# Sums of squared keys and queries: one four-pass fp32 product replaced by two one-pass products of a high and a low part

## The chip, the cores and the metric

The kernel runs on one core of one Trainium2 chip. The metric is device time in microseconds (us) of one launch; lower is better. The engines are TensorE (PE: matrix products, with its weight loads listed as PEld), VectorE (DVE), ScalarE (ACT), GpSimd (POOL) and SyncE (SP, which issues most DMAs). Each has its own instruction queue that is worked in order, and they meet only at semaphores.

## The reference, cut to what matters

One encoder layer over 512 tokens (two groups of 256) with 1024 channels. The change sits in the first stage, which projects the normed input, convolves, applies SiLU, and L2-normalises keys and queries of the gated delta net, 8 heads of 128 channels each.

```python
n1 = rmsnorm(h, W['norm_mix'][i])
proj = n1 @ W['w_in'][i]
...
qkv = jax.nn.silu(centred_depthwise_conv(qkv, conv_w).astype(f32))
q, k, v = jnp.split(qkv, 3, axis=-1)
...
def l2norm(t):
    return t * lax.rsqrt(jnp.sum(t * t, axis=-1, keepdims=True) + EPS)
...
q, k, v = l2norm(heads(q)), l2norm(heads(k)), heads(v)
```

After it come a state-space mixer, the gated delta net, an expert feed-forward and an output gate, none of which the change touches.

## The kernel before, in words

The program is a row of stages (project, ssd, gdn, then the expert stages), each a block in which the five engines run side by side, with a barrier of all engines at its end. Only `project_stage` is changed.

In it the 5120 convolved channels are 40 tiles `t` of 128 channels, each `128 x 512` (channels on the partitions, tokens along the row). A pair of tiles shares one 128x2048 weight chunk. Exact fp32 products are avoided: every operand is split into a high part (`fp32r`, a rounded fp32 that TensorE takes in one pass) and a low part (the rest), and `products` adds high*high, low*high and high*low, 8 k-tiles times 3, so 24 matrix instructions for a tile (L180 to L182). The queues in one iteration `t` are written out by hand:

- **TensorE**: the 24 products of tile `t` into PSUM bank `t % 4`; then, for a key or query tile (head `k`, tiles 8 to 15 for `k` 0 to 7 and 24 to 31 for `k` 8 to 15), the sum of its squares, `LAG` = 2 tiles late (after product 10 for head 0, and so on): L517 multiplies the squares with a 0/1 column of `column_strip`, which adds the 128 channels of head `k` into row `k % 8` of PSUM bank 4. Then `spreads` (L492, the inverse norms sent back to all partitions) and the transposes of finished tiles (L536), where there are any.
- **ScalarE**: waits for product `t`, writes the centre tap of the convolution (L587); on odd `t` it then makes the high part of a coming weight chunk (L545, `split`); then SiLU of tile `t-1` (L557) and, for a head's tile, its squares (L563, into one of two slots of `squares_of`). So the head that follows a `split` is always an even `k`.
- **GpSimd**: makes the low part of each weight chunk as soon as its high part is there: L460, `w_low = w_slots - w_high`, one instruction of 128x2048, once in two tiles.
- **VectorE**: in iteration `t` copies a transposed tile (L649), scales a head by its inverse norm (L654), then waits for the centre tap and adds the three other taps (L683). Once for the keys and once for the queries it takes the reciprocal (L666) and makes the low part of the inverse norms (L669, a subtraction of two tiles in SBUF).

Of the kernel before, what the change touches and what calls it, by code (L numbers as in the profile page):

```python
# [7 lines left out]
ACT = mybir.ActivationFunctionType  # L8
AX = mybir.AxisListType
F32 = mybir.dt.float32  # L10
F32R = mybir.dt.float32r
U32 = mybir.dt.uint32

P = 128
SEQS = 2
L = 256
T = SEQS * L
# [99 lines left out]
def bits32(x):  # L117

    return x.bitcast(F32)
# [8 lines left out]
AT_XT, AT_OG, AT_CH, AT_WORK, AT_END = 57.25, 73.25, 89.25, 169.25, 222.5  # L128
# [199 lines left out]
def project_stage(nc, m):  # L328
# [10 lines left out]
    NH = GDN_H  # L339
    SQUARED = 2  # L340
    LAG = 2
# [4 lines left out]
    small_r, w_r, split_r = m.region(AT_XT, AT_OG), m.region(AT_OG, AT_CH), m.region(AT_WORK, AT_END - 4.25)  # L346
# [3 lines left out]
    wsh, wsl = small_r.take("w_small_high", [P, KT, 64], F32R), small_r.take("w_small_low", [P, KT, 64], F32R)  # L350
    tab = small_r.take("a_coefficients", [P, 48])
    small_t = small_r.take("small_t", [64, T])
    s2 = split_r.take("squares_of", [P, SQUARED, T])
    wh, wl = split_r.take("w_high", [P, 2, KT, CC], F32R), split_r.take("w_low", [P, 2, KT, CC], F32R)
    norms = split_r.take("norms_of", [P, T])
    norms_h, norms_l = (split_r.take(f"norms_{x}", [P, T], F32R) for x in ("high", "low"))
    strip = split_r.take("column_strip", [P, NH - 1 + P])
    rows = split_r.take("row_selectors", [P, NH, P], F32R)
    w_in = [m.sem(f"w_slot{j}_loaded") for j in range(2)]
    part_in = [m.sem(f"w_first{h}_loaded") for h in range(2)]  # L360
# [8 lines left out]
    squared, summed, rooted, inverted, spread, scaled = (  # L369
        m.sem(x) for x in ("qk_squared", "qk_summed", "qk_rooted", "qk_inverted", "qk_spread", "qk_scaled"))  # L370
    split_h, split_l = m.sem("norms_high_done"), m.sem("norms_low_done")
    made, zeroed = m.sem("selectors_made"), m.sem("strip_zeroed")
    turned, copied = m.sem("turned"), [m.sem(f"turned_copied_{x}") for x in ("act", "dve")]
    par = m.colp[:, COL_CONV:COL_MIX].rearrange("p (c k) -> p c k", k=5)
# [24 lines left out]
    def head_of(t):  # L399

        for n, c in enumerate(FIRST):
            if c <= t < c + NH:
                return n * NH + t - c
        return None
# [10 lines left out]
    with nc.Block() as block:  # L415
# [30 lines left out]
        @block.gpsimd  # L446
        def _(pool):
            pool.memset(m.eps[:, :], EPS)
            pool.memset(strip[:, :], 0.0).then_inc(zeroed, 1)
            pool.wait_ge(zeroed, 1)  # L450
            pool.memset(strip[:, NH - 1:NH], 1.0).then_inc(made, 1)
            for h in range(2):
                ks = slice(h * HALF, (h + 1) * HALF)
                pool.wait_ge(part_high, h + 1)
                pool.tensor_tensor(wl[:, 0, ks, :], w[:, 0, ks, :], bits32(wh[:, 0, ks, :]), ALU.subtract).then_inc(part_low, 1)
            pool.wait_ge(small_high, 1)
            pool.tensor_tensor(wsl[:, :, :], ws[:, :, :], bits32(wsh[:, :, :]), ALU.subtract).then_inc(small_low, 1)
            for c in range(1, CHUNKS):
                pool.wait_ge(high, c)
                pool.tensor_tensor(wl[:, c % 2, :, :], w[:, c % 2, :, :], bits32(wh[:, c % 2, :, :]), ALU.subtract).then_inc(low, 1)  # L460
                if c == 4:
                    pool.wait_ge(eye_in, 16)
                    pool.tensor_copy(rows[:, :, :], sq(m, "eye")[:, 0:NH].unsqueeze(2).broadcast_to([P, NH, P])).then_inc(made, 1)

        @block.tensor
        def _(pe):
            def tile_product(t, ready=lambda k: None):
                j = (t // 2) % 2
                f = slice((t % 2) * P, (t % 2 + 1) * P)
                if t >= 2 and t % 2 == 0:  # L470
                    pe.wait_ge(low, t // 2)
                if t >= BANKS:
                    pe.wait_ge(conv, t - BANKS + 1)
                products(pe, m.ps[:, t % BANKS, :], [(wh[:, j, k, f], wl[:, j, k, f]) for k in range(KT)],
                         [(m.nh[:, k, :], m.nl[:, k, :]) for k in range(KT)], ready).then_inc(prod, 1)

            def first(k):
                pe.wait_ge(norm.out_done, k + 1)
                if k % HALF == 0:
                    pe.wait_ge(part_low, k // HALF + 1)  # L480

            def spreads(t):
                for n in spreads_behind(t):
                    if n == 0:
                        pe.wait_ge(made, 2)
                        pe.wait_ge(act_small, 1)
                    if n % NH == 0:
                        pe.wait_ge(split_l, n // NH + 1)
                    if n >= 1:
                        pe.wait_ge(scaled, n if n <= NH else n - 1)  # L490
                    for last, part in enumerate((norms_h, norms_l)):
                        ins = pe.matmul(m.ps[:, spread_bank(n), :], rows[:, n % NH, :], part[:, :], start=last == 0, stop=last == 1)  # L492
                    ins.then_inc(spread, 1)

            pe.wait_ge(eye_in, 16)
            norm.pe(pe)
            for t in range(N_CONV):
                tile_product(t, first if t == 0 else lambda k: None)
                if t == 1:
                    pe.wait_ge(small_low, 1)  # L500
                    products(pe, m.ps[0:64, 6, :], [(wsh[:, k, :], wsl[:, k, :]) for k in range(KT)],
                             [(m.nh[:, k, :], m.nl[:, k, :]) for k in range(KT)]).then_inc(small_prod, 1)
                if t == 2:
                    pe.wait_ge(small_staged, 1)
                    for tt in range(TT):
                        last = pe.transpose(m.ps[:, 7, tt * 64:(tt + 1) * 64], small_t[:, tt * P:(tt + 1) * P], sq(m, "eye")[0:64, 0:64])
                    last.then_inc(small_turned, 1)
                k = head_of(t - LAG)
                if k is not None:

                    if k == 0:
                        pe.wait_ge(made, 1)
                    if k == NH:
                        pe.wait_ge(rooted, 1)
                    pe.wait_ge(squared, k + 1)
                    j = k % NH
                    pe.matmul(m.ps[:, 4, :], strip[:, NH - 1 - j:NH - 1 - j + P], s2[:, k % SQUARED, :], start=j == 0,  # L517
                              stop=j == NH - 1).then_inc(summed, 1)
                if t == DECAYS_AT:
                    pe.wait_ge(const_in, 32)  # L520
                    pe.wait_ge(dve_small, 1)
                    g = m.decay[:, :, 32:48]
                    for n, mask in enumerate(("le", "ge", "gt", "lt")):
                        last = pe.matmul(m.ps[:, 5, n * 64:(n + 1) * 64], sq(m, mask), g, start=True, stop=True)
                    last.then_inc(gate_out, 1)
                spreads(t)
                for g in turns_behind(t):
                    base, _, half, tt = turn(g)
                    if base == CH_K:
                        pe.wait_ge(scaled, 4 * half + 4)  # L530
                    else:
                        pe.wait_ge(active, base + 4 * half + 4)
                    if g >= 2:
                        pe.wait_ge(copied[g % 2], g // 2)
                    for a in range(4):
                        last = pe.transpose(m.ps[:, 6 + g % 2, a * P:(a + 1) * P],  # L536
                                            m.ch[:, base + half * 4 + a, tt * P:(tt + 1) * P], sq(m, "eye"))
                    last.then_inc(turned, 1)
            spreads(N_CONV)

        @block.scalar
        def _(act):
# [11 lines left out]
            def silu(t):  # L554
                ct = m.ch[:, t, :]
                act.wait_ge(conv, t + 1)
                act.activation(ct, ct, ACT.Silu).then_inc(active, 1)  # L557
                k = head_of(t)
                if k is not None:
                    act.wait_ge(active, t + 1)  # L560
                    if k >= SQUARED:
                        act.wait_ge(summed, k - SQUARED + 1)
                    act.activation(s2[:, k % SQUARED, :], ct, ACT.Square).then_inc(squared, 1)  # L563

            def copies(t):
                for g in turns_behind(t):
# [47 lines left out]
        def _(dve):  # L614
# [43 lines left out]
            for t in range(N_CONV):  # L658
# [17 lines left out]
                        scale(n)  # L676
                y = m.ch[:, t, :].rearrange("p (s l) -> p s l", l=L)
                x = m.ps[:, t % BANKS, :].rearrange("p (s l) -> p s l", l=L)
                dve.wait_ge(taps0, t + 1)
                for n, (k, lo, hi) in enumerate(((0, 2, 0), (1, 1, 0), (3, 0, 1))):  # L680
                    yy = y[:, :, lo:L - hi]
# [1845 lines left out]
```

## Time and profile before

| what | value |
|---|---|
| median of 3 runs | 2313.6 us (2307.98 to 2319.12) |
| the profiled execution's own time | 2303.59 us |
| its span, first to last instruction | 2301.7 us |
| TensorE busy over the span | 98% |
| mean granted TensorE clock | 0.996 of full speed |

How to read it: the profile comes from one execution, whose own time is 1.9 us above its span. It is 0.4% below the median of the three timed runs. Busy shares are averages over stages that have different limits.

### The profile page before, as it was taken

To read this page: it belongs to the slowest core of one execution; us is meant where nothing else is said; L and a number is where in the kernel's file an instruction comes from. 1 tells how busy PE (TensorE), PEld (TensorE's weight loads), DVE (VectorE), ACT (ScalarE), POOL (GpSimd) and SP (SyncE) were. 2 spreads that over 40 slices of the span, in tenths; PEclk is the share of its full clock that TensorE was granted. 3 is DMA by queue.
4 is the path that set the end of the run, shared out by engine and by line. 5 is a ranking of instruction groups with operands and counts; after the bars stand their busy time and mean duration, and the time that the engine had idled before them with its cause. 6 is when DMAs were issued, how large, how long until landed. Compare 5 with 4: busy or idle time off the path is not lost.

```text
span 2301.7 us, 31020 instructions
## 1 busy us (share of the span) xinstructions
PE 2246.4 (98%) x10876; PEld 1873.3 (81%) x10876; DVE 1489.4 (65%) x3500; ACT 909.0 (39%) x1449; POOL 1098.3 (48%) x885
## 2 busy tenths in 40 slices
PE   8999899899989999999999999999999999999998
PEld 6787788788888888888888888888888888888885
DVE  4544566567654353068888888883239887878783
ACT  6454465344443333243333333333323333333343
POOL 3433232445424333426666666666527766555600
PEclk9999999999999999999999999999999999999999
DMA  4222011254424332234444444446478999999940
GB/s 170 81 84 75 27 56 47 95 181 160 133 75 149 110 110 110 73 98 141 151 140 149 143 146 147 142 151 228 161 251 330 388 373 364 345 362 346 362 171 37
DMA packets 160321, 394.71 MB, mean 171 GB/s; under 512 B 27376, under 2 KB 93168, under 8 KB 149872
## 3 DMA queue, kind: packets, MB, share of 16 engines
q1 hardware_dynamic: 125424, 326.32, 40.8%
q0 software_dynamic: 34816, 67.41, 8.0%
q8 instruction: 38, 0.62, 0.1%
q14 instruction: 43, 0.35, 0.1%
HBM read 328.45 MB, written 65.21 MB: 171 GB/s over the span
## 4 chain that ended last, share of the span: by engine, by line
PE 68%; DVE 1%; ACT 1%; DMA 1%; issue 0%; POOL 0%; DVEq 0%; POOLq 0%
PE ps L1331 13%; PE ps L182 11%; PE ps L180 11%; PE ps L181 11%; PE ps L2391 7%; PE ps L2393 7%; PE ps L2392 7%; PE ps L1664 1%; PE ps L2443 1%; DMA down_picked_gelu_sb<-a_dense,chosen_gelu_at_sb 0%; DMA a_dense<-up_gelu_sb 0%; POOL down_picked_gelu_sb L2123 0%; PE ps L1414 0%; PE ps L2421 0%; ACT ffn_norm_scaled_sb L1555 0%
## 5 line engine op out<-in xcount | busy, mean ns | idle before, releaser
L1912 POOL DMA_INDIRECT g_dense<-up_gates_summed_sb,up_gate_at_sb x384 | 415.5, 1082 | 265.5 <-issue 222.0
L180 PE MATMUL ps<-n_high_sb,up_u_high_sb 128*128 128x512 f32 x1024 | 398.4, 389 | 0.0
L182 PE MATMUL ps<-n_high_sb,up_u_low_sb 128*128 128x512 f32 x1024 | 398.4, 389 | 0.0
L181 PE MATMUL ps<-n_low_sb,up_u_high_sb 128*128 128x512 f32 x1024 | 398.3, 389 | 0.0
L2391 PE MATMUL ps<-down_v_high_sb,down_w_high_sb 128*128 128x512 f32 x768 | 298.9, 389 | 0.6 <-DVE down_w_low_sb L2167 0.6
L2393 PE MATMUL ps<-down_v_high_sb,down_w_low_sb 128*128 128x512 f32 x768 | 298.8, 389 | 0.0
L2392 PE MATMUL ps<-down_v_low_sb,down_w_high_sb 128*128 128x512 f32 x768 | 298.8, 389 | 0.0
L1755 DVE TENSOR_TENSOR up_u_low_sb<-up_u_sb,up_u_high_sb 128x1024 fp32r<-128x1024 f32 x128 | 156.3, 1222 | 143.6 <-ACT up_u_high_sb L1931 143.2
L2311 ACT ACTIVATE down_v_high_sb<-down_v_sb 128x1024 fp32r<-128x1024 f32 x120 | 125.8, 1048 | 309.5 <-PE ps L2393 292.5
L1943 ACT ACTIVATE up_gelu_sb<-ps 128x512 f32<-128x512 f32 x128 | 76.5, 598 | 406.3 <-PE ps L182 406.2
L2133 POOL DMA_INDIRECT expert_rows_sb<-expert_v,chosen_expert_sb x128 | 157.0, 1227 | 158.5 <-DVE h_sb L2183 59.2
L182 PEld LDWEIGHTS ps<-n_high_sb,up_u_low_sb 128*128 128x128 f32 x1024 | 192.2, 188 | 40.0
L181 PEld LDWEIGHTS ps<-n_low_sb,up_u_high_sb 128*128 128x128 f32 x1024 | 192.2, 188 | 39.9
L180 PEld LDWEIGHTS ps<-n_high_sb,up_u_high_sb 128*128 128x128 f32 x1024 | 192.2, 188 | 39.8
L2165 DVE TENSOR_TENSOR down_v_low_sb<-down_v_sb,down_v_high_sb 128x1024 fp32r<-128x1024 f32 x124 | 151.3, 1220 | 84.4 <-ACT down_v_high_sb L2311 70.5
L2123 POOL DMA_INDIRECT down_picked_gelu_sb<-a_dense,chosen_gelu_at_sb x128 | 148.3, 1159 | 72.2 <-issue 71.4
L2391 PEld LDWEIGHTS ps<-down_v_high_sb,down_w_high_sb 128*128 128x128 f32 x768 | 144.1, 188 | 30.8 <-DVE down_v_low_sb L2165 1.0
L2393 PEld LDWEIGHTS ps<-down_v_high_sb,down_w_low_sb 128*128 128x128 f32 x768 | 144.1, 188 | 30.0
L2392 PEld LDWEIGHTS ps<-down_v_low_sb,down_w_high_sb 128*128 128x128 f32 x768 | 144.1, 188 | 29.9
L683 DVE SCALAR_TENSOR_TENSOR channels_sb<-ps,column_params_sb,channels_sb 128x510 f32<-128x510 f32 (+1 forms) x120 | 89.3, 747 | 117.5 <-ACT channels_sb L587 114.6
L460 POOL TENSOR_TENSOR w_low_sb<-w_slots_sb,w_high_sb 128x2048 fp32r<-128x2048 f32 x19 | 87.5, 4605 | 142.8 <-ACT w_high_sb L545 142.8
L1294 POOL TENSOR_TENSOR merge_low_sb<-merge_slots_sb,merge_high_sb 128x2048 fp32r<-128x2048 f32 x18 | 83.8, 4657 | 147.7 <-ACT merge_high_sb L1289 147.7
(360 smaller groups left out, 4616.0 us busy)
## 6 DMA issues: line engine op xcount, KB each, us to landing
up_u_sb<-expert_u SPq DMA_DIRECT2D x128, 512.0 KB, 3.9
down_v_sb<-expert_v SPq DMA_DIRECT2D x32, 2048.0 KB, 12.0
a_dense<-up_gelu_sb SPq DMA_DIRECT2D x128, 256.0 KB, 2.2
g_dense<-nought_sb SPq DMA_DIRECT2D x8, 3072.0 KB, 11.2
down_gelu_sb<-a_dense SPq DMA_DIRECT2D x32, 768.0 KB, 4.8
down_gates_sb<-g_dense SPq DMA_DIRECT2D x32, 768.0 KB, 6.3
w_slots_sb<-w_conv SPq DMA_DIRECT2D x19, 1024.0 KB, 4.8
query_slots_sb<-peer_query SPq DMA_DIRECT2D x8, 1024.0 KB, 6.0
```

What stands on the lines that cost most here:

```text
L180: pe.matmul(out, ah, bh, start=k == 0, stop=False)
L181: pe.matmul(out, ah, bl, start=False, stop=False)
L182: last = pe.matmul(out, al, bh, start=False, stop=k == n - 1)
L1331: last = pe.matmul(m.ps[:, banks + f, :], a[u], b[v], start=kt == 0 and n == 0, stop=kt == KT - 1 and n == 2)
L1755: dve.tensor_tensor(ul[:, n, :, :], u[:, n, :, :], bits32(uh[:, n, :, :]), ALU.subtract).then_inc(low, 1)
L1912: pool.indirect_dma_start(cells, at, summed[:, tt, k:k + 1], None).then_inc(stored[tt], 16)
L2123: pool.indirect_dma_start(picked[:, u, k:k + 1], None, gelus, at).then_inc(gelu_in[n % 2], 16)
L2133: pool.indirect_dma_start(m.rows[:, s, :], None, experts, at).then_inc(row_in[s], 16)
L2165: dve.tensor_tensor(vl[b][:, j, :], v[:, b, j, :], bits32(vh[b][:, j, :]), ALU.subtract).then_inc(v_low, 1)
L2391: pe.matmul(m.ps[:, q, :], wh[b][:, j, t], vh[b][:, j, c], start=start, stop=False)
L2392: pe.matmul(m.ps[:, q, :], wh[b][:, j, t], vl[b][:, j, c], start=False, stop=False)
L2393: return pe.matmul(m.ps[:, q, :], wl[b][:, j, t], vh[b][:, j, c], start=False, stop=stop)
```

## The change

For each head, ScalarE now makes a high part of the squares (`squares_high`, fp32r) right behind the squares, and VectorE makes the low part (`squares_low`, which lies in the same place as `squares_of`), before it adds the taps of the next tile but one. TensorE then runs two one-pass products in place of one fp32 product, and it waits for the low part instead of for the squares. The strip of selector columns becomes fp32r. `squares_high` lies where the input tokens were, which are no longer needed. GpSimd's only edits are the bit views of two memsets.

```diff
+    s2_low = m.region(AT_WORK, AT_WORK + 4).take("squares_low", [P, SQUARED, T], F32R)
     s2 = split_r.take("squares_of", [P, SQUARED, T])
+    s2_high = m.h_region().take("squares_high", [P, SQUARED, T], F32R)
...
-    strip = split_r.take("column_strip", [P, NH - 1 + P])
+    strip = split_r.take("column_strip", [P, NH - 1 + P + 25], F32R)
...
-                    pe.wait_ge(squared, k + 1)
+                    pe.wait_ge(squared_l, k + 1)
                     j = k % NH
-                    pe.matmul(m.ps[:, 4, :], strip[:, NH - 1 - j:NH - 1 - j + P], s2[:, k % SQUARED, :], start=j == 0,
-                              stop=j == NH - 1).then_inc(summed, 1)
+                    column = strip[:, NH - 1 - j:NH - 1 - j + P]
+                    pe.matmul(m.ps[:, 4, :], column, s2_high[:, k % SQUARED, :], start=j == 0, stop=False)
+                    pe.matmul(m.ps[:, 4, :], column, s2_low[:, k % SQUARED, :], start=False, stop=j == NH - 1).then_inc(summed, 1)
...
                     act.activation(s2[:, k % SQUARED, :], ct, ACT.Square).then_inc(squared, 1)
+                    act.wait_ge(squared, k + 1)
+                    act.activation(s2_high[:, k % SQUARED, :], s2[:, k % SQUARED, :], ACT.Copy).then_inc(squared_h, 1)
...
                 x = m.ps[:, t % BANKS, :].rearrange("p (s l) -> p s l", l=L)
+                k = head_of(t - LAG)
+                if k is not None:
+                    dve.wait_ge(squared_h, k + 1)
+                    j = k % SQUARED
+                    dve.tensor_tensor(s2_low[:, j, :], s2[:, j, :], bits32(s2_high[:, j, :]), ALU.subtract).then_inc(squared_l, 1)
                 dve.wait_ge(taps0, t + 1)
```

TensorE's queue behind the product of tile 30, before (the sum of the squares of head 12):

```order
L180 MATMUL ps<-n_high_sb,w_high_sb 128x512
L181 MATMUL ps<-n_low_sb,w_high_sb 128x512
L182 MATMUL ps<-n_high_sb,w_low_sb 128x512
L517 MATMUL ps<-squares_of_sb,column_strip_sb 128x512
L536 MATMUL ps<-squares_sb,channels_sb 128x128 x4
L180 MATMUL ps<-n_high_sb,w_high_sb 128x512
```

And the same place in the changed kernel:

```order
L180 MATMUL ps<-n_high_sb,w_high_sb 128x512
L181 MATMUL ps<-n_low_sb,w_high_sb 128x512
L182 MATMUL ps<-n_high_sb,w_low_sb 128x512
L521 MATMUL ps<-squares_high_sb,column_strip_sb 128x512
L522 MATMUL ps<-squares_low_sb,column_strip_sb 128x512
L540 MATMUL ps<-squares_sb,channels_sb 128x128 x4
L180 MATMUL ps<-n_high_sb,w_high_sb 128x512
```

Nothing moved past anything; one row became two, and the transposes (`squares_sb` is there the table of constant squares, its identity) follow as before.

ScalarE's queue in the odd iteration 29 and the even iteration 30 of the changed kernel, where the squares of heads 12 and 13 are made:

```order
L593 ACTIVATE channels_sb<-ps,column_params_sb 128x512
L549 ACTIVATE w_high_sb<-w_slots_sb 128x2048
L561 ACTIVATE channels_sb<-channels_sb 128x512
L567 ACTIVATE squares_of_sb<-channels_sb 128x512
L569 ACTIVATE squares_high_sb<-squares_of_sb 128x512
L593 ACTIVATE channels_sb<-ps,column_params_sb 128x512
L561 ACTIVATE channels_sb<-channels_sb 128x512
L567 ACTIVATE squares_of_sb<-channels_sb 128x512
L569 ACTIVATE squares_high_sb<-squares_of_sb 128x512
```

L569 is the only kind of row added; L549 is the `split` that GpSimd waits for, and it still stands ahead of the squares of the even head.

VectorE's queue in the same stretch of the changed kernel: the taps of tile 29, a copy of a transposed tile, and then iteration 30.

```order
L694 SCALAR_TENSOR_TENSOR channels_sb<-ps,column_params_sb,channels_sb 128x2x254
L694 SCALAR_TENSOR_TENSOR channels_sb<-ps,column_params_sb,channels_sb 128x2x255 x2
L655 COPY channels_sb<-ps 128x512
L689 TENSOR_TENSOR squares_low_sb<-squares_of_sb,squares_high_sb 128x512
L694 SCALAR_TENSOR_TENSOR channels_sb<-ps,column_params_sb,channels_sb 128x2x254
L694 SCALAR_TENSOR_TENSOR channels_sb<-ps,column_params_sb,channels_sb 128x2x255 x2
```

The subtraction L689 of head 12 stands ahead of the taps of tile 30, and TensorE waits for it behind the product of tile 30.

## Rows read from the trace of the kernel before

**Rows 1.** The page's head: the span, and busy time of each engine.
```profile
span 2301.7 us, 31020 instructions
PE 2246.4 (98%) x10876; PEld 1873.3 (81%) x10876; DVE 1489.4 (65%) x3500; ACT 909.0 (39%) x1449; POOL 1098.3 (48%) x885
```

**Rows 2.** Busy time in windows: the project stage's tiles, then ssd and gdn.
```profile
30.00:278.00 248.00, 244.89 (x1099) 195.35 (x1097) 129.11 (x170) 115.19 (x144) 84.01 (x19) 1.00 0.21 72
...
280.00:780.00 500.00, 474.96 (x2939) 415.58 (x2940) 305.58 (x615) 233.60 (x551) 198.20 (x197) 0.99 0.33 110
```

**Rows 3.** Timeline (start, length, instruction) of TensorE: an fp32 sum, and a pair of one-pass products.
```profile
214.36 1.02 PE L517 MATMUL ps<-squares_of_sb,column_strip_sb 128*128 128x512 f32 x2
...
215.21 0.27 PE L536 MATMUL ps<-squares_sb,channels_sb 128*128 128x128 f32 x1
...
154.43 0.39 PE L492 MATMUL ps<-norms_high_sb,row_selectors_sb 128*128 128x512 f32 x1
154.66 0.39 PE L492 MATMUL ps<-norms_low_sb,row_selectors_sb 128*128 128x512 f32 x1
154.89 0.40 PE L180 MATMUL ps<-n_high_sb,w_high_sb 128*128 128x512 f32 x1
```

**Rows 4.** Timeline of ScalarE in iteration 29, and its copy of one 128x512 high part.
```profile
208.45 1.91 ACT L545 ACTIVATE w_high_sb<-w_slots_sb 128x2048 fp32r<-128x2048 f32 x1
...
210.91 0.63 ACT L563 ACTIVATE squares_of_sb<-channels_sb 128x512 f32<-128x512 f32 x1
...
147.24 0.61 ACT L605 ACTIVATE norms_high_sb<-norms_of_sb 128x512 fp32r<-128x512 f32 x1
```

**Rows 5.** Timeline of VectorE behind iteration 29, its copy.
```profile
210.82 0.68 DVE L649 COPY channels_sb<-ps 128x512 f32<-128x512 f32 x1
```

**Rows 6.** Timeline of GpSimd's and VectorE's subtractions that meet (two cases).
```profile
145.46 4.61 POOL L460 TENSOR_TENSOR w_low_sb<-w_slots_sb,w_high_sb 128x2048 fp32r<-128x2048 f32 x1 [7.17 <-ACT w_high_sb L545]
...
147.88 2.74 DVE L669 TENSOR_TENSOR norms_low_sb<-norms_of_sb,norms_high_sb 128x512 fp32r<-128x512 f32 x1 [1.70 <-ACT norms_high_sb L605]
...
250.26 4.61 POOL L460 TENSOR_TENSOR w_low_sb<-w_slots_sb,w_high_sb 128x2048 fp32r<-128x2048 f32 x1 [8.12 <-ACT w_high_sb L545]
...
252.68 2.74 DVE L669 TENSOR_TENSOR norms_low_sb<-norms_of_sb,norms_high_sb 128x512 fp32r<-128x512 f32 x1 [1.96 <-ACT norms_high_sb L605]
```

**Rows 7.** One line's instructions: a VectorE subtraction of 1024 columns (min/median/max ns).
```profile
L742 DVE TENSOR_TENSOR ssd_gate_low_sb<-ssd_gate_w_sb,ssd_gate_high_sb x8: 1226/1310/2040, 286.2 to 388.5; 128x1024 fp32r<-128x1024 f32 x8
```

**Rows 8.** GpSimd's subtraction beside heads 0, 6, 8, 10, 12, then the sums of four.
```profile
81.67 4.59 POOL L460 TENSOR_TENSOR w_low_sb<-w_slots_sb,w_high_sb 128x2048 fp32r<-128x2048 f32 x1 [4.26 <-ACT w_high_sb L545]
...
121.04 4.59 POOL L460 TENSOR_TENSOR w_low_sb<-w_slots_sb,w_high_sb 128x2048 fp32r<-128x2048 f32 x1 [8.52 <-ACT w_high_sb L545]
...
182.38 4.59 POOL L460 TENSOR_TENSOR w_low_sb<-w_slots_sb,w_high_sb 128x2048 fp32r<-128x2048 f32 x1 [8.15 <-ACT w_high_sb L545]
195.99 4.61 POOL L460 TENSOR_TENSOR w_low_sb<-w_slots_sb,w_high_sb 128x2048 fp32r<-128x2048 f32 x1 [9.02 <-ACT w_high_sb L545]
210.44 4.61 POOL L460 TENSOR_TENSOR w_low_sb<-w_slots_sb,w_high_sb 128x2048 fp32r<-128x2048 f32 x1 [9.84 <-ACT w_high_sb L545]
...
84.74 0.59 PE L517 MATMUL ps<-squares_of_sb,column_strip_sb 128*128 128x512 f32 x1
...
124.50 0.59 PE L517 MATMUL ps<-squares_of_sb,column_strip_sb 128*128 128x512 f32 x1
...
185.89 0.59 PE L517 MATMUL ps<-squares_of_sb,column_strip_sb 128*128 128x512 f32 x1
...
200.35 0.59 PE L517 MATMUL ps<-squares_of_sb,column_strip_sb 128*128 128x512 f32 x1
```

**Rows 9.** Timeline where TensorE restarts behind a wait for VectorE.
```profile
15.86 0.75 DVE L299 SCALAR_TENSOR_TENSOR n_low_sb<-ps,column_params_sb,n_high_sb 128x512 fp32r<-128x512 f32 x1 [2.97 <-ACT n_high_sb L275]
...
16.66 0.50 PE L180 MATMUL ps<-n_high_sb,w_high_sb 128*128 128x512 f32 x1 [0.94 <-DVE n_low_sb L299]
17.00 0.40 PE L181 MATMUL ps<-n_low_sb,w_high_sb 128*128 128x512 f32 x1
```

More of the change, by code:

```diff
@@ L371, in project_stage @@
     split_h, split_l = m.sem("norms_high_done"), m.sem("norms_low_done")
+    squared_h, squared_l = m.sem("qk_squares_high"), m.sem("qk_squares_low")
     made, zeroed = m.sem("selectors_made"), m.sem("strip_zeroed")
@@ L448, in _ @@
             pool.memset(m.eps[:, :], EPS)
-            pool.memset(strip[:, :], 0.0).then_inc(zeroed, 1)
+            pool.memset(bits32(strip[:, :]), 0.0).then_inc(zeroed, 1)
             pool.wait_ge(zeroed, 1)
-            pool.memset(strip[:, NH - 1:NH], 1.0).then_inc(made, 1)
+            pool.memset(bits32(strip[:, NH - 1:NH]), 1.0).then_inc(made, 1)
             for h in range(2):
```

## The prediction

> **What bounds the kernel now.** I read the head of the page first. TensorE is busy 2246.4 of 2301.7 us [rows 1], so what it does not have to do, or has to wait for, shows in the end time nearly one for one. Since this is a mean over stages, I then took the busy time in a window over the stage that changes: in 30 to 278 us TensorE is busy 244.89 of 248.00 us, VectorE 129.11, ScalarE 115.19 and GpSimd 84.01 [rows 2]. The other engines have half their time free, and TensorE's queue is back to back. The stage ends with a barrier, so a shift of its end moves all later stages rigidly; nothing behind it can take the shift up.
>
> **What is removed.** Sixteen fp32 products with the selector strip, one for a head. One takes two records; the next instruction starts 215.21 - 214.36 = 0.85 us behind it [rows 3]. In its place come two one-pass products of the same shape. The pair L492 shows what these cost: 154.89 - 154.43 = 0.46 us for two, 0.23 each [rows 3]. So a head gives back 0.85 - 0.46 = 0.40 us (0.39 by the rounded rows; where the follower is a one-pass product the change of mode adds a few hundredths, so I take 0.40), and 16 heads 6.4 us. That is the whole possible gain, 0.28% of the span.
>
> **What is added beside it.** ScalarE gets 16 copies of 128x512, 0.61 us each by the like copy L605 [rows 4], 9.8 us in all; ScalarE is idle over 130 us of the window [rows 2], and the centre tap, on which VectorE waits, stands ahead of the copy in its queue. I cost the copies at nothing by themselves. VectorE gets 16 subtractions of 128x512. Alone, a subtraction of 1024 columns takes 1.23 us (the least of eight [rows 7]), so one of 512 takes some 0.6 to 0.65 us; 10 us in all, beside 119 us in which VectorE is idle. Bare work costs nothing either. What may cost is *when* the subtraction can run, since TensorE now waits for it.
>
> **Where the even heads stand.** Take head 12. In iteration 29 ScalarE makes the high part of the weights until 208.45 + 1.91 = 210.36, then SiLU, then the squares from 210.91 [rows 4]. The new copy follows (0.65 us later, the spacing of such dependent steps) and ends near 212.2. VectorE is done with its copy at 210.82 + 0.68 = 211.50 [rows 5], so its subtraction can start at about 212.2. But GpSimd started its 4.61 us subtraction of the weights at 210.44 and holds on until 215.05 [rows 8]. Both read two tiles of SBUF. The trace has two cases in which VectorE's L669, the same operation in the same form and size, meets this very instruction: it starts at 147.88, takes 2.74 us and ends at 150.62, where GpSimd ended at 145.46 + 4.61 = 150.07; and again it starts at 252.68 and ends at 255.42, where GpSimd ended at 254.87 [rows 6]. Both times it ends 0.55 us behind GpSimd, four times its own length after its start. So I read it as blocked until GpSimd is through. The new subtraction will be too, in every even head, since the weights' split stands in front of the squares in ScalarE's queue and GpSimd begins with the split's end, 1.7 us ahead.
>
> The Trainium skill (SBUF — State Buffer, Who interferes with whom) says the same as a rule: a VectorE instruction with two SBUF inputs contends with a GpSimd instruction that reads SBUF, and the one that is issued second is fully blocked until the first is done. By that rule the bare 0.6 us price of the subtraction would be wrong and the even heads would wait; the trace agrees, with the two ends 0.55 us behind GpSimd's.
>
> **What that costs TensorE.** TensorE reaches the sum of an even head at the start of L517, less 0.40 us, because the odd head in front of it was cheaper (not for heads 0 and 8, which have none in front). The low part is there 0.55 us after GpSimd's end. Then TensorE restarts: at L299 the producer ends at 15.86 + 0.75 = 16.61, and the second product behind the wait starts at 17.00 [rows 9], which without a wait would be 0.23 behind the first; so the effective start is 17.00 - 16.61 - 0.23 = 0.16 us behind the producer's end. The stall is therefore (GpSimd's end - start of L517) + 0.55 + 0.16, and + 0.40 where a cheaper sum came before. The first bracket from [rows 8] and, for head 12, the L517 of [rows 3]:
>
> head 0: 86.26 - 84.74 = 1.52, stall 2.23;
> head 6: 125.63 - 124.50 = 1.13, stall 2.24;
> head 8: 186.97 - 185.89 = 1.08, stall 1.79;
> head 10: 200.60 - 200.35 = 0.25, stall 1.36 (it has the spreads and the transposes in front, which give it time);
> head 12: 215.05 - 214.36 = 0.69, stall 1.80; heads 2, 4 and 14 repeat this within 0.02 us, so four times 1.80.
>
> Sum: 2.23 + 2.24 + 1.79 + 1.36 + 7.20 = 14.8 us.
>
> **The odd heads** cost nothing. In an even iteration there is no split; the copy is done some 2.7 us behind the centre tap's start, VectorE has the taps behind it about 1 to 2 us later (the blocked subtraction makes them at most that late), GpSimd is idle, and TensorE comes to the odd head's sum more than 5 us after the centre tap's start. That late tap is the thing that is next in line: VectorE starts the taps of an even tile some 0.6 to 1 us later than now. TensorE needs them four tiles on, ScalarE's SiLU one tile on, so both are covered by a tile of 5.4 us (24 products of 0.23).
>
> **Sum.** -6.4 + 14.8 = +8.4 us. The profiled execution of before took 2303.6 us, so such an execution takes 2312.0. That execution was 10 us below the median of the runs shown; on the median, 2313.6 + 8.4 = 2322.0 us. It is 0.36% slower. I call differences within 0.5% (11.6 us) the same, which is about what a measurement of this kernel can tell from no change; the three runs of before lie 0.5% apart.
>
> The bounds of the terms: the gain is 16 times 0.39 to 0.45, 6.2 to 7.2 us; the upper value holds if the mode change of TensorE costs more than the rows with a transpose behind them show. The part behind GpSimd's end is 0.55 us by two cases, 0.65 if nothing of the instruction was done ahead; the restart lies between 0.05 and 0.3 us. Eight times these give 14 to 17 us of stall. So the case by itself spans +6.8 to +10.8 us.
>
> **The rivals.**
>
> A, no block: the new subtraction runs beside GpSimd's, because something else delayed L669. Then the low part of head 12 is there at 212.9, 1.5 us before TensorE wants it, no head stalls, and the kernel is 6.4 us faster: 2307.2 us. For it: L742, also a subtraction, is mostly near its least time. Against it: L669's two ends sit at the same distance behind GpSimd's, and L742's longest is 2040 ns against 1226 [rows 7], so it can be delayed too. The case decides for itself if VectorE can begin ahead of GpSimd, which would need the copy 1.8 us earlier.
>
> B, TensorE's clock falls: eight pauses of some 2 us in a stage that had nearly none bring the granted clock down from 2.4 to 1.2 GHz for a while. Each tile at the lower clock costs 5.4 us more; one tile behind each pause would be 8 x 5.4 = 43 us on top, 2365 us. Above one tile in all it decides the sign beyond 0.5%. Against it: in 280 to 780 us TensorE is busy 474.96 of 500.00 us, 5% idle, and the granted clock is 0.99 there [rows 2]; here idle time would be 3.1 + 14.8 of 256 us, 7%.
>
> C, the stall is hidden: the stalled TensorE also delays the next split and so nothing is gained or lost beyond the pair of tiles. I don't believe that it closes: the split starts with the end of an odd tile's product, so GpSimd's end is tied to TensorE's own progress, 7.3 us behind it, and the pause comes anew in each pair. But if part of the pauses overlapped with work that TensorE waits for anyway (3.1 us of idle in the window), up to 3 us would come off: +5.4 us, 2319.0.
>
> **How the numbers follow.** My forecast (block, pauses of 1.4 to 2.2 us at even heads) has 0.86, C included; A 0.08; B 0.06. A is the one on the faster side, but its 0.28% is within the bound of the same. Of the forecast's share, some 0.1 falls above 0.5% by the bounds and the scatter of medians; with B that is 0.16 slower. Faster by over 0.5% would need A and a lucky scatter: 0.03. The rest, 0.81, is the same. For the range I take +5.4 to +10.8 around 2313.6 and some 5 us for the scatter of the median at the upper side and 6 at the lower: 2313 to 2330, 17 us wide, with the lower end drawn to 2312, which leaves out A and B.
>
> **What the profile after would show.** The sums' two records 0.23 us apart; a wait of TensorE for `squares_low` in eight places, 1.2 to 2.2 us each, 14 to 15 us in all, and none at odd heads; VectorE's subtraction near 3.4 us at even heads (from 212.2 to 215.6 for head 12), ending 0.55 us behind GpSimd's, and near 0.65 us at odd ones; the distance between centre taps longer by about 1.4 us (1.8 less 0.4) on one tile of each pair and shorter by 0.4 on the other; the next stage starting 8.4 us later. I am wrong if the subtraction at even heads is short (A), if the granted clock in the stage is below 0.97 (B), or if an odd head waits too, which would mean that a late tap is not covered.

## The result, and the profile after

The changed kernel takes 2315.13 us in the median of 23 runs, the kernel before 2306.07 us in the median of 23. The ratio of the paired comparison is 1.0034, 95% interval 1.0024 to 1.0044: slower by 0.34%, some 7.8 us (0.0034 x 2306). It was forecast at +8.4 us, 0.36%, and as "the same", with a chance of 0.81 for that and 0.16 for slower by over 0.5%.

Three of the 23 runs of the changed kernel had a mean granted clock of 0.64 to 0.85 (2528.88 to 3573.71 us) and are left out of the ratio; the first profile is of one of them, at full clock until about 2050 us and at 0.16 behind it, so only the project stage is read from it. A second profile of the same kernel, taken with the experiments, has a span of 2317.1 us and the same eight pauses within 0.04 us.

The busy time in the window that [rows 2] shows of before:

```profile
30.00:278.00 248.00, 235.19 (x1078) 191.26 (x1077) 154.61 (x178) 123.55 (x156) 84.03 (x19) 1.00 0.21 71
```

TensorE is busy 9.7 us less in the same 248 us, at the same full clock; in before it was idle for 3.1 us of them. VectorE is busy 25.5 us more, though 16 subtractions of 0.68 us make only 11 us. The list of waits of the first profile says who TensorE waits for (engine, line, waited for; us in total, times, longest), between 80 and 250 us:

```profile
PE ps L521 <- DVE squares_low_sb L689: 12.8, 8, 2.1
PEld ps L521 <- DVE squares_low_sb L689: 11.7, 6, 2.4
...
PEld ps L521 <- issue: 4.4, 2, 2.4
```

Eight times the first of the two new products waits for the low part. The weight load (PEld) is held up first and the product behind it, which is why both engines list the same pauses. One line's instructions, for VectorE's subtraction, from the second profile:

```profile
L689 DVE TENSOR_TENSOR squares_low_sb<-squares_of_sb,squares_high_sb x16: 680/2006/3347, 84.1 to 241.4; 128x512 fp32r<-128x512 f32 x16
```

The least and the greatest time are a factor of five apart for one form and size. The first profile again, the timeline of head 12 (iterations 29 and 30), the place for which the prediction gave its working:

```profile
216.89 4.59 POOL L463 TENSOR_TENSOR w_low_sb<-w_slots_sb,w_high_sb 128x2048 fp32r<-128x2048 f32 x1 [10.44 <-ACT w_high_sb L549]
...
218.02 0.63 ACT L569 ACTIVATE squares_high_sb<-squares_of_sb 128x512 fp32r<-128x512 f32 x1
...
218.69 3.35 DVE L689 TENSOR_TENSOR squares_low_sb<-squares_of_sb,squares_high_sb 128x512 fp32r<-128x512 f32 x1 [0.74 <-ACT squares_high_sb L569]
...
220.16 0.39 PE L182 MATMUL ps<-n_high_sb,w_low_sb 128*128 128x512 f32 x1
...
222.09 0.50 PE L521 MATMUL ps<-squares_high_sb,column_strip_sb 128*128 128x512 f32 x1 [1.55 <-DVE squares_low_sb L689]
222.43 0.40 PE L522 MATMUL ps<-squares_low_sb,column_strip_sb 128*128 128x512 f32 x1
222.67 0.27 PE L540 MATMUL ps<-squares_sb,channels_sb 128*128 128x128 f32 x1
...
224.18 0.68 DVE L689 TENSOR_TENSOR squares_low_sb<-squares_of_sb,squares_high_sb 128x512 fp32r<-128x512 f32 x1
...
228.35 0.39 PE L182 MATMUL ps<-n_high_sb,w_low_sb 128*128 128x512 f32 x1
228.58 0.40 PE L521 MATMUL ps<-squares_high_sb,column_strip_sb 128*128 128x512 f32 x1
228.81 0.39 PE L522 MATMUL ps<-squares_low_sb,column_strip_sb 128*128 128x512 f32 x1
229.04 0.27 PE L540 MATMUL ps<-squares_sb,channels_sb 128*128 128x128 f32 x1
```

The subtraction of head 12 starts 1.80 us after GpSimd's and ends at 218.69 + 3.35 = 222.04, which is 0.56 us behind GpSimd's end (221.48). Without the wait TensorE would have started L521 at 220.16 + 0.23 = 220.39; it starts at 222.09. Head 13, whose subtraction meets nothing, takes 0.68 us, and its L521 follows 0.23 us behind the last product, without a pause. The pair of new products is 0.46 us long there (229.04 - 228.58), against 0.85 for the fp32 one [rows 3].

To compare kernels in the stage, whatever the start of the run and the later stages do, I use the sum of two stretches, from the centre tap of tile 10 to that of tile 18 and from 26 to 34; each holds eight of the sums. The timeline of the changed kernel has these four taps:

```profile
84.44 0.78 ACT L593 ACTIVATE channels_sb<-ps,column_params_sb 128x512 f32<-128x512 f32 x1 [1.50 <-PE ps L182]
...
141.68 0.78 ACT L593 ACTIVATE channels_sb<-ps,column_params_sb 128x512 f32<-128x512 f32 x1 [2.79 <-PE ps L182]
...
190.52 0.78 ACT L593 ACTIVATE channels_sb<-ps,column_params_sb 128x512 f32<-128x512 f32 x1 [1.97 <-PE ps L182]
...
249.69 0.78 ACT L593 ACTIVATE channels_sb<-ps,column_params_sb 128x512 f32<-128x512 f32 x1 [3.28 <-PE ps L182]
```

57.24 + 59.17 = 116.4 us. The same taps in before stand at 84.94, 137.36, 186.09 and 241.67: 52.42 + 55.58 = 108.0 us. The difference is 8.4 us. The next stage's first instruction starts at 287.63 us, against 279.57, 8.1 us later, though tile 10's tap had come 0.5 us earlier than in before.

### The profile page after: what moved, and what is told of

Same layout as the page of the kernel before. It is cut to its first block, busy times and chain, and to the rows that moved or that the text cites. A ratio compares the mean times of both kernels' runs of the same rounds, so it can differ in the third digit from the quotient of the medians.

```text
span 3571.7 us, 31052 instructions
## 1 busy us (share of the span) xinstructions
PE 3503.6 (98%) x10876; PEld 2694.0 (75%) x10876; DVE 1521.3 (43%) x3516; ACT 921.0 (26%) x1465; POOL 1110.0 (31%) x885
## 4 chain that ended last, share of the span: by engine, by line
PE 80%; issue 1%; DVE 0%; ACT 0%; DVEq 0%
PE ps L2402 14%; PE ps L2403 14%; PE ps L2404 14%; PE ps L180 9%; PE ps L182 9%; PE ps L181 9%; PE ps L1342 8%; PE ps L2454 2%; PE ps L2432 1%; PE ps L1675 0%; PE ps L1425 0%; ACT ffn_norm_scaled_sb L1566 0%; DVE h_sb L1385 0%; PE ps L1608 0%; ACT merge_high_sb L1300 0%
## 5 line engine op out<-in xcount | busy, mean ns | idle before, releaser
L2402 PE MATMUL ps<-down_v_high_sb,down_w_high_sb 128*128 128x512 f32 x768 | 679.8, 885 | 0.0
L2404 PE MATMUL ps<-down_v_high_sb,down_w_low_sb 128*128 128x512 f32 x768 | 679.8, 885 | 0.0
L2403 PE MATMUL ps<-down_v_low_sb,down_w_high_sb 128*128 128x512 f32 x768 | 679.7, 885 | 0.0
L1923 POOL DMA_INDIRECT g_dense<-up_gates_summed_sb,up_gate_at_sb x384 | 426.6, 1111 | 258.4 <-issue 213.8
L2404 PEld LDWEIGHTS ps<-down_v_high_sb,down_w_low_sb 128*128 128x128 f32 x768 | 356.0, 464 | 137.9 <-issue 119.2
L2403 PEld LDWEIGHTS ps<-down_v_low_sb,down_w_high_sb 128*128 128x128 f32 x768 | 355.7, 463 | 136.9 <-issue 118.4
L2402 PEld LDWEIGHTS ps<-down_v_high_sb,down_w_high_sb 128*128 128x128 f32 x768 | 355.3, 463 | 137.1 <-issue 118.6
L1942 ACT ACTIVATE up_u_high_sb<-up_u_sb 128x1024 fp32r<-128x1024 f32 x128 | 134.8, 1054 | 38.6 <-DMA up_u_sb<-expert_u 37.2
```

The source lines that it names most:

```text
L1923: pool.indirect_dma_start(cells, at, summed[:, tt, k:k + 1], None).then_inc(stored[tt], 16)
L2402: pe.matmul(m.ps[:, q, :], wh[b][:, j, t], vh[b][:, j, c], start=start, stop=False)
L2403: pe.matmul(m.ps[:, q, :], wh[b][:, j, t], vl[b][:, j, c], start=False, stop=False)
L2404: return pe.matmul(m.ps[:, q, :], wl[b][:, j, t], vh[b][:, j, c], start=False, stop=stop)
```

## The experiments

They ran in three batches on three chips, each beside the kernel before on the same chip, and every ratio is to the runs of before in its own batch. The theory: VectorE's subtraction with both inputs in SBUF can't run beside GpSimd's subtraction, which reads SBUF too; it waits for that instruction's end, and TensorE waits for it. The rival: the low part is late because of a longer chain (ScalarE's copy, then a subtraction that is slow by nature).

| kernel | two stretches, us | pauses of TensorE at the sums | ratio, 95% interval |
|---|---|---|---|
| before | 108.0 | 0 | 1 |
| changed | 116.4 | 8, 14.1 us | 1.0034, 1.0024 to 1.0044 |
| changed, again | 118.0 | 8, 14.0 us | 1.0039, 1.0025 to 1.0052 |
| split made, not used | 108.0 | 0 | 0.9996, 0.9984 to 1.0008 |
| high part only | 101.5 | 0 | 0.9973, 0.9961 to 0.9986 |
| GpSimd in pieces | 102.0 | 2, 0.3 us | 0.9961, 0.9947 to 0.9975 |
| squares of the keys in PSUM | 108.3 | 4, 6.3 us | 1.0001, 0.9992 to 1.0010 |
| one tile later | (shifted) | 8, 13.5 us | 1.0045, 1.0032 to 1.0059 |
| squares first | 101.5 | 0 | 0.9983, 0.9974 to 0.9992 |
| squares first, heads only | 101.5 | 0 | 0.9965, 0.9951 to 0.9979 |

A pause is counted here as the start of the sum's first product behind the last product's start, less the 0.23 us that it takes without a wait (for head 12, 222.09 - 220.16 - 0.23 = 1.70).

**The change again.**

> The changed kernel again, for a profile at full clock and a time beside the kernel before. Theory (port): eight pauses of TensorE at the even heads, 1.2 to 2.2 us each, 14 us in all, VectorE's subtraction 3.3 us at even and 0.68 us at odd heads; the ssd stage starts at 287.6 us, 8.1 us later than before; ratio 1.0035. Rival (long chain: the low part is late because ScalarE's copy and a subtraction that is slow by nature come behind each other): the same times here; the runs below tell them apart.

The time and the pauses came out so: 2315.77 us in the median, eight pauses of 2.22, 1.69, 1.67, 2.14, 1.75, 1.23, 1.67 and 1.68 us, the even subtractions 3.33 to 3.35 us and the odd ones 0.68. The next stage did not: it starts at 290.32 us and not at 287.6. Of these 2.7 us, 1.1 lie ahead of the sums (tile 9's tap at 79.61 us, 78.51 in the first profile), and the stretches are 1.6 us longer; the last section says why.

**Both halves of the change by themselves.** First the added work without its use:

```diff
+    h_r = m.h_region()
+    s2_high = h_r.take("squares_high", [P, SQUARED, T], F32R)
+    s2_low = h_r.take("squares_low", [P, SQUARED, T], F32R)
...
-                    pe.wait_ge(squared_l, k + 1)
+                    pe.wait_ge(squared, k + 1)
...
-                    pe.matmul(m.ps[:, 4, :], column, s2_high[:, k % SQUARED, :], start=j == 0, stop=False)
-                    pe.matmul(m.ps[:, 4, :], column, s2_low[:, k % SQUARED, :], start=False, stop=j == NH - 1).then_inc(summed, 1)
+                    pe.matmul(m.ps[:, 4, :], column, s2[:, k % SQUARED, :], start=j == 0, stop=j == NH - 1).then_inc(summed, 1)
```

> ScalarE's copies and VectorE's subtractions are made as in the change, but into a place of their own, and TensorE runs the fp32 product of the unsplit squares as before and waits for these only. Output unchanged. Theory (port): the subtractions are still 3.3 us at even heads, VectorE's taps of even tiles start 0.6 to 1 us later, TensorE has no pause; ssd starts at 279.6 us, ratio 1.000. Rival (the added work as such costs, on ScalarE or through late taps): later than 280.5 us, 1.001 or more.

The timeline of VectorE at the same two heads:

```profile
212.14 3.35 DVE L690 TENSOR_TENSOR squares_low_sb<-squares_of_sb,squares_high_sb 128x512 fp32r<-128x512 f32 x1 [0.73 <-ACT squares_high_sb L570]
215.41 2.30 DVE L695 SCALAR_TENSOR_TENSOR channels_sb<-ps,column_params_sb,channels_sb 128x508 f32<-128x508 f32 x3
217.63 0.68 DVE L690 TENSOR_TENSOR squares_low_sb<-squares_of_sb,squares_high_sb 128x512 fp32r<-128x512 f32 x1
```

The blocked subtraction is there unchanged, and VectorE's taps of tile 30 follow only behind it. Yet the two stretches take 108.01 us, against 108.00 before, and the ratio is 0.9996. So 16 copies, 16 subtractions and late taps cost nothing; only TensorE's wait for the low part does. Two things came out otherwise than expected. The taps behind the eight blocked subtractions are 0 to 1.0 us late here (0.1 to 1.0 in the change), not 0.6 to 1. And the next stage starts at 280.00 us, not at 279.6, still ahead of the rival's 280.5; the stage's tail behind tile 34 takes 38.4 us in place of 37.9, as it does in the next kernel, which makes no low part at all.

Then the gain without the subtraction; the low part of the squares is left out and the high part added twice:

```diff
-                    pe.wait_ge(squared_l, k + 1)
+                    pe.wait_ge(squared_h, k + 1)
...
-                    pe.matmul(m.ps[:, 4, :], column, s2_low[:, k % SQUARED, :], start=False, stop=j == NH - 1).then_inc(summed, 1)
+                    pe.matmul(m.ps[:, 4, :], column, s2_high[:, k % SQUARED, :], start=False, stop=j == NH - 1).then_inc(summed, 1)
...
-                    dve.tensor_tensor(s2_low[:, j, :], s2[:, j, :], bits32(s2_high[:, j, :]), ALU.subtract).then_inc(squared_l, 1)
```

> Two one-pass products as in the change, but both with the high part; VectorE makes no low part. The low part of the squares is left out of the sums (the high part is added twice). Theory (port): no pauses, since the high part of an even head is there 1.9 us ahead of TensorE; ssd starts 6.4 us earlier than before, at 273.2 us, ratio 0.997. If the one-pass products give back less than 0.40 us a head, it starts later than that. Rival (long chain): part of the pause stays, some 0.5 us at the heads 0, 6 and 8, where TensorE comes earliest.

No head pauses, and the stretches take 101.5 us, 6.45 less than before: 16 times 0.40. ScalarE's copy is in time at every head, which takes away half of the rival's chain. The next stage started at 273.89 us and not at 273.2; 0.5 of that is in the stage's tail behind tile 34, which takes 38.4 us here against 37.9.

**GpSimd's instruction in four pieces.**

```diff
-                pool.tensor_tensor(wl[:, c % 2, :, :], w[:, c % 2, :, :], bits32(wh[:, c % 2, :, :]), ALU.subtract).then_inc(low, 1)
+                for q in range(4):
+                    ks = slice(2 * q, 2 * q + 2)
+                    ins = pool.tensor_tensor(wl[:, c % 2, ks, :], w[:, c % 2, ks, :], bits32(wh[:, c % 2, ks, :]), ALU.subtract)
+                ins.then_inc(low, 1)
```

> The changed kernel with GpSimd's weight subtraction of 128x2048 issued as four of 128x512 (1.05 to 1.3 us each). Theory (port, held for one instruction): VectorE's subtraction gets in behind the piece that runs, so it ends at most 1.3 + 0.55 us after its start, ahead of TensorE in every head; no pause, or under 0.4 us at heads 0 and 6; ssd starts at 273.2 to 274 us, ratio 0.997. GpSimd takes 0.5 to 1 us longer for a chunk. Rival (subtraction slow by nature, or slowed by GpSimd's traffic for as long as that lasts): the subtraction stays near 3 us and the pauses stay, ssd at 287 us or later, 1.0035.

The timeline at head 12: GpSimd's four pieces merged into one row, then its second and third by themselves:

```profile
206.22 5.50 POOL L465 TENSOR_TENSOR w_low_sb<-w_slots_sb,w_high_sb 128x512 fp32r<-128x512 f32 x4 [8.17 <-ACT w_high_sb L552]
...
207.48 1.29 POOL L465 TENSOR_TENSOR w_low_sb<-w_slots_sb,w_high_sb 128x512 fp32r<-128x512 f32 x1
...
208.02 1.30 DVE L692 TENSOR_TENSOR squares_low_sb<-squares_of_sb,squares_high_sb 128x512 fp32r<-128x512 f32 x1 [0.73 <-ACT squares_high_sb L572]
...
208.73 1.73 POOL L465 TENSOR_TENSOR w_low_sb<-w_slots_sb,w_high_sb 128x512 fp32r<-128x512 f32 x1
```

VectorE's subtraction starts 1.80 us after GpSimd's first piece, as in the change, but takes 1.30 us in place of 3.35. It starts inside the second piece and ends at 209.32, 0.55 us behind that piece's end (208.77), the distance that it has behind the one long instruction in the change. GpSimd goes on until 211.72, 2.4 us after it is done. So VectorE is not slowed for as long as GpSimd works; it waits for one instruction. Then GpSimd is held in turn: its third piece takes 1.73 us, the second 1.29. The pauses shrink from 14.1 us to 0.18 at head 0 and 0.11 at head 6, the two at which TensorE comes earliest. The data and the sums are the same as in the change, so a subtraction that is slow by nature is out. The next stage starts at 274.14 us, 0.14 beyond the expected span.

**One input from PSUM.**

```diff
+    def squares_at(k):
+        return m.ps[:, 5, :] if k < NH and k % 2 == 0 else s2[:, k % SQUARED, :]
...
+                    act.activation(squares_at(k), ct, ACT.Square).then_inc(squared, 1)
...
+                    dve.tensor_tensor(s2_low[:, j, :], squares_at(k), bits32(s2_high[:, j, :]), ALU.subtract).then_inc(squared_l, 1)
```

> The changed kernel, but for the even heads of the keys (0, 2, 4, 6) ScalarE puts the squares in a PSUM bank, so that VectorE's subtraction has one input in PSUM and one in SBUF, at the same time beside the same GpSimd instruction. The queries' heads are as in the change and serve as the control. Theory (port, two SBUF inputs): the subtraction of heads 0 to 6 takes about 0.7 us, their pauses (7.7 us) vanish, those of heads 8 to 14 (6.4 us) stay; the stretch of taps 10 to 18 takes 49.5 us, that of 26 to 34 takes 59.2 us; ratio 1.000. Rival (VectorE is held by any work of GpSimd, or the position in the queues does it): all eight pauses stay, 1.0035.

One line's instructions:

```profile
L692 DVE TENSOR_TENSOR squares_low_sb<-squares_of_sb,squares_high_sb x12: 680/682/3358, 87.6 to 230.8; 128x512 fp32r<-128x512 f32 x12
L692 DVE TENSOR_TENSOR squares_low_sb<-ps,squares_high_sb x4: 690/692/692, 83.1 to 120.4; 128x512 fp32r<-128x512 f32 x4
```

The timeline of head 4:

```profile
106.36 4.63 POOL L466 TENSOR_TENSOR w_low_sb<-w_slots_sb,w_high_sb 128x2048 fp32r<-128x2048 f32 x1 [8.12 <-ACT w_high_sb L552]
...
108.09 0.69 DVE L692 TENSOR_TENSOR squares_low_sb<-ps,squares_high_sb 128x512 fp32r<-128x512 f32 x1 [0.67 <-ACT squares_high_sb L572]
```

At the same place in the queues, in the middle of the same 4.63 us of GpSimd, the subtraction with one input in PSUM takes 0.69 us and is through 2.2 us ahead of GpSimd. The first stretch takes 49.13 us (57.24 in the change), while the second, where both inputs are in SBUF, takes 59.15 us against 59.17, and its four pauses stand. This is the run that shows the cause: the second SBUF input.

**One tile later.**

```diff
-    SQUARED = 2
-    LAG = 2
+    SQUARED = 3
+    LAG = 3
```

> The changed kernel with LAG 3 in place of 2 and three slots: every sum, and the subtraction in front of it, one tile later, so the high part lies ready some 5 us before the subtraction. Theory (port): the subtraction of an odd head now falls beside GpSimd's, so the pauses stay, 14 us in all, but at the odd heads; the even heads have none; ratio 1.003 to 1.004 (some 1 us more from the later norms). Rival (the low part is late because of the chain ScalarE, copy, subtraction): no pause anywhere, ratio 0.997.

The timeline of head 1:

```profile
86.67 0.63 ACT L569 ACTIVATE squares_high_sb<-squares_of_sb 128x512 fp32r<-128x512 f32 x1
...
93.25 4.61 POOL L463 TENSOR_TENSOR w_low_sb<-w_slots_sb,w_high_sb 128x2048 fp32r<-128x2048 f32 x1 [7.22 <-ACT w_high_sb L549]
...
94.23 4.17 DVE L689 TENSOR_TENSOR squares_low_sb<-squares_of_sb,squares_high_sb 128x512 fp32r<-128x512 f32 x1
...
98.46 0.51 PE L521 MATMUL ps<-squares_high_sb,column_strip_sb 128*128 128x512 f32 x1 [1.52 <-DVE squares_low_sb L689]
```

The high part is ready at 87.30, seven microseconds ahead of the subtraction, and there is a pause all the same: all eight odd heads pause (1.23 to 2.16 us, 13.5 in all) and no even head does. More slack in front of the subtraction does not help, since VectorE comes to it 1.0 us after GpSimd has begun (0.4 to 1.6 us over the eight heads). The ratio of 1.0045 is a little above the expected 1.003 to 1.004, which its interval takes in. The next stage starts 1.3 us later than in the change (288.94 against 287.63 us); I put that down to the norms, which are a tile later, without a run of its own.

**The order turned, so that VectorE comes first.**

```diff
+                if t:
+                    silu(t - 1)
                 if t % 2 == 1 and t // 2 + 2 < CHUNKS:
                     split(t // 2 + 2)
-                if t:
-                    silu(t - 1)
```

and the subtraction stands first in VectorE's iteration.

> The changed kernel with two rows moved: on ScalarE the SiLU, squares and high part of tile t-1 stand ahead of the split of the weights, and on VectorE the subtraction stands first in its iteration. Theory (port): the subtraction starts some 1.5 us before GpSimd's, takes 0.68 us in all 16 heads, and GpSimd, which starts about 2 us later than in the change, is still ahead of TensorE's need. No pause; the stretch of centre taps 10 to 18 and 26 to 34 takes 101.5 us (108.0 before, 116.4 after), ratio 0.997. Rival (the weights' low part gets late, or the new order makes the norms' chain later): pauses of TensorE at the products of even tiles instead.

All 16 subtractions take 0.68 to 0.74 us, no sum pauses, and the stretches take 101.5 us, as expected. But the ratio is 0.9983, some 4 us, where the kernel with the high part only gained 6. The rival that I had named takes some 2 us of it: at the start of the stage the weights' low part is late. The timeline has one new wait, and how it comes about:

```profile
62.45 0.63 ACT L561 ACTIVATE channels_sb<-channels_sb 128x512 f32<-128x512 f32 x1 [5.81 <-DVE channels_sb L694]
...
64.96 4.59 POOL L463 TENSOR_TENSOR w_low_sb<-w_slots_sb,w_high_sb 128x2048 fp32r<-128x2048 f32 x1 [12.20 <-ACT w_high_sb L549]
...
69.60 0.50 PE L180 MATMUL ps<-n_high_sb,w_high_sb 128*128 128x512 f32 x1 [2.00 <-POOL w_low_sb L463]
```

ScalarE stands in front of the SiLU of an early tile, for which VectorE's taps are late behind its work on the decays, and the split now queues behind that, GpSimd's subtraction behind the split, and TensorE's next product behind GpSimd. So I turned the order only at the heads' tiles:

```diff
+                early = t > 0 and head_of(t - 1) is not None
+                if early:
+                    silu(t - 1)
                 if t % 2 == 1 and t // 2 + 2 < CHUNKS:
                     split(t // 2 + 2)
-                if t:
+                if t and not early:
                     silu(t - 1)
```

> As the kernel with the squares first, but ScalarE's SiLU, squares and high part go ahead of the weights' split only where tile t-1 is a head's; everywhere else, the start of the stage above all, the order is that of the change. Theory (port): no pause, the two stretches of taps take 101.5 us together, and the centre tap of tile 9 stays at 78.5 to 79.2 us (81.3 where the order was turned everywhere), so ssd starts at 273.0 to 273.9 us, ratio 0.997. Rival (the new order itself costs 2 us, wherever it stands): ssd at 275.5 us again, 0.998.

No pause at the sums or at the start, 101.5 us for the stretches, and the next stage starts at 273.87 us, within the expected span and 1.7 us earlier than with the order turned everywhere, though tile 9's tap came at 79.5 us and not by 79.2. The kernel is faster than before: 0.9965. The intervals of the two orders overlap a little (0.9974 to 0.9992, 0.9951 to 0.9979), so their difference rests on the traces more than on the times. The grouped view of VectorE between 80 and 240 us shows the subtractions (busy us, mean ns):

```profile
L686 DVE TENSOR_TENSOR squares_low_sb<-squares_of_sb,squares_high_sb 128x512 fp32r<-128x512 f32 x16 | 11.0, 688 | 0.0
```

This version and the one with GpSimd in pieces beat both kernels; their intervals overlap, so the runs don't rank them.

## Where the prediction was right, and the step that failed

**The gain.** 0.40 us a head, 6.4 us in all. The kernel with the high part only gives 6.45 us in the stretches.

**The block.** Foreseen from L669 [rows 6]: an end 0.55 us behind GpSimd's. The sixteen profiled even heads (the first profile and the repeated one) have 0.545 to 0.554 us. What rested on two rows, and on the rule that the prediction cites from the Trainium skill, is now shown: one PSUM input takes the block away, and pieces shorten it to one piece. That a subtraction which begins first is not held stands in the trace of before, in the next stage:

```profile
286.22 1.23 DVE L742 TENSOR_TENSOR ssd_gate_low_sb<-ssd_gate_w_sb,ssd_gate_high_sb 128x1024 fp32r<-128x1024 f32 x1 [2.48 <-ACT ssd_gate_high_sb L738]
286.26 2.08 POOL L839 TENSOR_TENSOR decay_steps_high_sb<-decay_high_sb,squares_sb 128x512 fp32r<-128x512 f32 x1 [2.16 <-PE ps L872]
...
357.06 1.04 POOL L839 TENSOR_TENSOR decay_steps_high_sb<-decay_high_sb,squares_sb 128x512 fp32r<-128x512 f32 x1
357.15 2.04 DVE L742 TENSOR_TENSOR ssd_gate_low_sb<-ssd_gate_w_sb,ssd_gate_high_sb 128x1024 fp32r<-128x1024 f32 x1 [1.47 <-ACT ssd_gate_high_sb L738]
```

VectorE begins 0.04 us ahead in the first pair and takes its least time, and GpSimd's 1.04 us become 2.08; in the second pair GpSimd is ahead, and VectorE's 1.23 us become 2.04. These are two of the eight instructions that [rows 7] sums up. The four that are at their least time, which the prediction took as speaking for rival A, began ahead of GpSimd's (this one) or met none; the other four end 1.08 us behind the end of the GpSimd instruction that was ahead of them. The two kernels with the squares first do not test this, since their subtraction at a split is over before GpSimd's begins. The Trainium skill (SBUF — State Buffer, Who interferes with whom) also says that a VectorE instruction with at most one SBUF input, outside the two-port modes, does not contend with GpSimd; the run with the keys' squares in PSUM agrees, with 0.69 us beside GpSimd.

**The stall.** 14.8 us forecast, 14.1 measured: 2.21, 1.68, 1.67, 2.14, 1.75, 1.24, 1.70, 1.68 for the even heads against 2.23, 1.80, 1.80, 2.24, 1.79, 1.36, 1.80, 1.80. Of the restart, 0.16 us forecast, only 0.05 shows as a pause (222.09 - 222.04); the rest sits behind it, in the distance of the pair (222.43 - 222.09 = 0.34 and not 0.23). Over the eight heads that distance adds 0.8 us, so the stall is 14.9 us, and less the 6.45 us of gain it is 8.45, against 8.4 in the stretches.

**The odd heads and the late taps.** No odd head pauses, and the kernel with the split made but not used shows that taps up to 1.0 us late are free. The distances between centre taps went as forecast, longer by 1.0 to 1.9 us at the even heads (1.4 at five of the eight) and shorter by 0.4 at the odd ones.

**The rivals.** A (no block) is excluded: 0.9973 would have been its ratio, as the run with the high part only shows. B (the clock) did not happen in the stage of the first profile, granted clock 1.00; in the repeated one it did for 3.4 us (mean 0.99 in the stage), last section. C, that part of the pauses would be hidden, is not seen.

**The step that failed: what counts as the same.** The prediction said: "I call differences within 0.5% (11.6 us) the same, which is about what a measurement of this kernel can tell from no change; the three runs of before lie 0.5% apart." On that it gave 0.81 to the same and only 0.16 to slower, though its own sum was +8.4 us. The step takes the spread of single executions for the uncertainty of a comparison. The runs showed that a comparison is about five times finer: with 23 runs a side the ratio is 1.0034 with an interval of 1.0024 to 1.0044, and the repetition gives 1.0039, 1.0025 to 1.0052. A ratio of 1 lies outside both, so the kernel is slower, and by the amount that the sum gave.

**The base.** The forecast of 2322.0 us stood on the three runs of before with their median of 2313.6; with 23 runs that median is 2306.07. This term was 7.5 us too high, nearly as much as the change itself, and so is most of the 6.9 us between forecast and result; 2306.07 + 8.4 = 2314.5 us is beside the measured 2315.13. By its terms alone the prediction's range would have begun at 2313.6 + 5.4 = 2319.0 us; the measured time lies inside 2312 to 2330 only through the 6 us left for the scatter of the median, and not by the reckoning. The difference of two medians, 9.1 us, and the paired ratio, 7.8, lie on both sides of the forecast.

## What to carry to other kernels

Before an engine is made to wait for a VectorE instruction with two SBUF inputs, look in the trace at what GpSimd runs at that moment: the price is not the instruction's length but the rest of GpSimd's, if GpSimd was first. It can be avoided in three ways that all worked here: keep one of the inputs in PSUM, cut GpSimd's instruction into pieces, or order the queues so that VectorE begins first, only where it is needed. Giving the producer a tile more of time did not help, because the collision is set by the order of the queues, not by slack.

## What the runs showed that I had not expected

In the repeated profile of the change the stretch of taps 10 to 18 was 1.6 us longer than in the first. Windows around the place (length, busy time of the engines, granted clock, DMA share, GB/s):

```profile
128.00:131.00 3.00, 1.02 (x6) 0.52 (x5) 3.00 (x2) 2.22 (x4) 2.06 (x1) 1.00 0.00 0
131.60:135.00 3.40, 3.40 (x10) 2.65 (x9) 1.79 (x3) 0.00 (x0) 0.00 (x0) 0.50 0.66 280
```

One microsecond after the pause at head 6 (it ends at 130.66 us) TensorE's granted clock fell to 0.50, the lower of its two levels, for 3.4 us, and the products came 0.43 us apart in place of 0.23, which makes up the 1.6 us. It is my rival B in small: one drop behind 28 pauses for the low part in four profiles (8 and 8 in the change, 8 with the sums one tile later, 4 with the keys' squares in PSUM); the other 27 passed without it. Whether the pause or something else set it off stays open.

A second surprise: how far a 0.68 us subtraction can stretch. The same form took 1.30 us with GpSimd in pieces, 3.35 us in the change and up to 4.75 us with the sums one tile later, by nothing but what GpSimd was in the middle of.
